# Transformer layer on one core: the shared expert of token tiles 6 and 7 computed behind the expert loop, and the first expert's list between the halves of a product

## What is computed

```python
h = layer_norm(DEEPNORM_ALPHA * h + mix, ln1_g[l], ln1_b[l])
ffn = moe_ffn(h, ...)
h = layer_norm(DEEPNORM_ALPHA * h + ffn, ln2_g[l], ln2_b[l])

def moe_ffn(h, w_router, router_bias, wg, wu, wd, sg, su, sd):
    idx, w = route(xf, w_router, router_bias)          # 6 of 64 experts for each token
    routed = routed_experts(xf, idx, w, wg, wu, wd)    # each expert: (silu(x wg) * (x wu)) wd, weighted
    shared = (jax.nn.silu(xf @ sg) * (xf @ su)) @ sd   # hidden width 256, every token
    return routed + shared
```

## Time and profile before

| | us |
|---|---|
| median of three runs | 2063.84 |
| fastest and slowest of them | 2063.03, 2066.24 |
| the profiled execution's own time | 2066.02 |
| its span, first to last instruction | 2064.2 |
| TensorE busy | 1989.3 (96%) |
| VectorE busy | 1136.6 (55%) |
| GpSimd busy | 777.1 (38%) |
| ScalarE busy | 505.2 (24%) |
| mean granted TensorE clock | 0.989 |

### The profile page before, as it was taken

The page is one execution under the profiler, slowest core; times in us unless marked ns, Lnnn a source line. Parts: engine busy times, 40 slices in busy tenths (PEclk is TensorE's granted clock), DMA queues, the critical chain, the costliest instruction groups (busy, mean ns, idle before and its releaser), DMA issues.

```text
span 2064.2 us, 23774 instructions
## 1 busy us (share of the span) xinstructions
PE 1989.3 (96%) x7237; PEld 1004.3 (49%) x7238; DVE 1136.6 (55%) x3065; ACT 505.2 (24%) x1102; POOL 777.1 (38%) x717
## 2 busy tenths in 40 slices
PE   8999999999999999999999999999999999999991
PEld 6444667575544444444445554444444444444440
DVE  6222546776611222235676656966666656666645
ACT  3111554452322222224432230111111111111113
POOL 1762005612122222115980003554554545454531
PEclk9999999999999999999999999999999999999996
DMA  5421000011141222144353006999999999999964
GB/s 147 132 87 41 21 21 22 22 47 47 46 138 69 74 77 77 57 130 161 111 202 141 31 32 260 369 364 359 360 360 354 364 346 354 347 342 352 337 206 171
DMA packets 129639, 370.45 MB, mean 179 GB/s; under 512 B 33712, under 2 KB 65668, under 8 KB 103832
## 3 DMA queue, kind: packets, MB, share of 16 engines
q1 hardware_dynamic: 103960, 314.83, 41.1%
q0 software_dynamic: 23520, 54.61, 10.5%
q10 hardware_dynamic: 2080, 0.01, 0.1%
HBM read 320.57 MB, written 68.17 MB: 188 GB/s over the span
## 4 chain that ended last, share of the span: by engine, by line
PE 25%; DMA 21%; issue 4%; POOL 3%; DVE 2%; POOLq 0%; ACT 0%; SPq 0%; DVEq 0%
DMA sums<-arena,row_to 21%; PE banks L3193 8%; PE banks L2289 4%; PE banks L3209 3%; PE banks L2336 3%; POOL arena L2136 2%; PE banks L2014 2%; PE banks L279 1%; PE banks L2352 1%; PE banks L2312 1%; DMA arena<-in_w_router_dram 0%; DVE arena L3269 0%; PE banks L3201 0%; DVE arena L3186 0%; PE banks L2299 0%
## 5 line engine op out<-in xcount | busy, mean ns | idle before, releaser
L3193 PE MATMUL banks<-arena 128*128 128x512 f32 x1056 | 466.6, 595 | 4.1 <-issue 3.5
L3172 POOL DMA_INDIRECT arena<-h_rows,index x268 | 281.0, 1048 | 140.2 <-issue 78.7
L3193 PEld LDWEIGHTS banks<-arena 128*128 128x128 f32 x1056 | 196.6, 191 | 227.7 <-issue 227.6
L1720 PE MATMUL banks<-arena 128*128 128x512 f32 x672 | 298.8, 594 | 0.4 <-ACT arena L323 0.4
L3209 PE MATMUL banks<-arena 128*128 128x512 f32 x528 | 237.5, 592 | 1.4 <-ACT arena L3008 0.9
L3180 POOL DMA_INDIRECT sums<-arena,row_to x66 | 106.2, 1609 | 275.9 <-DMA sums<-arena,row_to 242.2
L279 PE MATMUL banks<-arena 128*128 128x512 f32 x416 | 193.5, 602 | 2.3 <-PEq L108 2.2
L1720 PEld LDWEIGHTS banks<-arena 128*128 128x128 f32 x672 | 123.2, 190 | 134.7 <-issue 134.7
L3156 DVE TENSOR_SCALAR index<-row 32x1 uint32<-32x1 f32 x1072 | 155.4, 145 | 17.1
L3209 PEld LDWEIGHTS banks<-arena 128*128 128x128 f32 x528 | 100.2, 190 | 127.1 <-issue 125.3
L3186 DVE STREAM_TRANSPOSE arena<-arena 128x1024 f32<-128x1024 f32 x66 | 133.7, 2026 | 48.9 <-PE banks L3193 47.2
(11 more groups left out here) (400 smaller groups left out, 2420.0 us busy)
## 6 DMA issues: line engine op xcount, KB each, us to landing
arena<-in_w_exp_gate_dram SPq DMA_DIRECT2D x66, 1024.0 KB, 6.4
arena<-in_w_exp_up_dram SPq DMA_DIRECT2D x66, 1024.0 KB, 10.7
arena<-in_w_exp_down_dram SPq DMA_DIRECT2D x66, 1024.0 KB, 13.5
arena<-in_w_in_dram SPq DMA_DIRECT2D x26, 1024.0 KB, 5.4
gates<-arena SPq DMA_DIRECT2D x60, 256.0 KB, 2.0
arena<-gates SPq DMA_DIRECT2D x15, 1024.0 KB, 7.7
arena<-h_rows,index POOLq DMA_INDIRECT x268
arena<-in_x_dram SPq DMA_DIRECT2D x8, 512.0 KB, 5.6
```

What stands on the lines that cost most here:

```text
L1720: mm = pe.matmul(gate_bank(n, b), left[:, k, :], right[:, k, :], start=(alone and k == 0), stop=(k == 3), skip_group_check=True)
L3172: return pool.indirect_dma_start(w.x[k][:, 256 * q:256 * (q + 1)], None, rows, bass.IndirectOffsetOnAxis(ap=g.index[:, k, q:q + 1], axis=0 ...
L3193: mm = pe.matmul(g.bank[:, 2, :].rearrange("p (a f) -> p a f", a=2), xT[:, k, :], wgu[:, :, k, :], start=(k == 0), stop=(k == KT - 1))
```

## The change

Tiles 6 and 7 (`EARLY` = 6 and up) have their shared expert no longer ahead of the expert loop but in `finish`.

- `up`, `turn_hidden`, `down` on TensorE, `gate`, `turned_hidden` on ScalarE and `hidden`, `sum_base` on VectorE are gone for these tiles. `last_down` and `last_sum` are now those of tile 5.
- In their place ScalarE multiplies the rows of tiles 6 and 7 by ALPHA (`scale`, two instructions), and SyncE stores these. The order of the stores changes to 0, 1, 2, 3, 6, 7, 4, 5. Those of tiles 0 and 1 signal `kept_free`, the other six `sums_begun`.
- The turned rows of tiles 6 and 7 must live until the end. They are written to the rows of tiles 0 and 1 in `base` (`late_turned`), so `turned(6)` and `turned(7)` wait for `kept_free`. The shared weights stay too. The overflow tables and the gain and bias rows of the last normalisation, which lay over the weights, move over other rows of `base`. So VectorE waits for all six stores (`sums_begun`) before each quarter of `overflow_tables`, and SyncE waits for them before the loads of gain and bias.
- The list of expert 0 stands between the two halves of `up(5)`; `index(0)` comes before `hidden(5)`. List 3 moves from before the first product of expert 0 to behind it, and step 0 on VectorE is written in another order: it turns the rows of expert 1 and makes `hidden` first, then index 3 and select 4.
- In `finish` TensorE computes both `up` as soon as it has left the loops, then for each late tile `turn_hidden`, the tile's rows of `sums` times the identity into the banks, and `down` added to them. ScalarE reads the sum of tiles 6 and 7 out of the banks. Its Silu, and copies of the turned hidden product, stand between the normalisation of the tiles.

```diff
 LAG = 3
+EARLY = NT - 2
+KEPT = BASE
+TABLES = BASE + 2 * D
...
         def begin_sum(m):
-            sp.wait_ge(s["base"], m + 1)
-            sp.dma_start(g.sums[m * P:(m + 1) * P, :], base[:, m, :]).then_inc(g.sums_begun, 16)
+            if m < EARLY:
+                sp.wait_ge(s["base"], m + 1)
+            else:
+                sp.wait_ge(s["scaled"], m - EARLY + 1)
+            sp.dma_start(g.sums[m * P:(m + 1) * P, :], base[:, m, :]).then_inc(
+                kept_free[m] if m < NT - EARLY else g.sums_begun, 16)
...
-        for m in range(NT - DELAY - 1, NT - 2):
+        begin_sum(NT - DELAY - 1)
+        for m in range(EARLY, NT):
             begin_sum(m)
-        sp.wait_ge(s["gu"], NT)
+        sp.wait_ge(s["gu"], EARLY)
         load_expert(g, sp, 2)
-        begin_sum(NT - 2)
-        sp.wait_ge(s["dn"], NT)
+        begin_sum(EARLY - 2)
+        sp.wait_ge(s["dn"], EARLY)
         load_expert(g, sp, 3)
-        begin_sum(NT - 1)
+        begin_sum(EARLY - 1)
...
-        up(5)
+        up(5, range(0, KT // 2))
         lists(0)
+        up(5, range(KT // 2, KT))
         down(4)
         turn_hidden(5)
-        up(6)
         lists(1)
-        down(5)
-        turn_hidden(6)
-        up(7)
         lists(2)
-        down(6)
-        turn_hidden(7)
-        first.last_down = lambda: down(NT - 1)
+        first.last_down = lambda: down(EARLY - 1)
...
+        index(0)
         hidden(5)
-        index(0)
         select(1)
         sum_base(4)
-        hidden(6)
         index(1)
         select(2)
-        sum_base(5)
         turned_first()
+        index(2)
         select(3)
-        hidden(7)
-        index(2)
-        sum_base(6)
-        first.last_sum = lambda: sum_base(NT - 1)
+        first.last_sum = lambda: sum_base(EARLY - 1)
...
+            if m >= EARLY:
+                act.wait_ge(kept_free[m - EARLY], 16)
...
+        def scale(m):
+            act.wait_ge(h1_stored[m], 16)
+            act.activation(base[:, m, :], base[:, m, :], ACT.Copy, scale=ALPHA).then_inc(s["scaled"], 1)
...
+        for m in range(EARLY, NT):
+            scale(m)
         turned_hidden(4)
         gate(5)
         turned_hidden(5)
-        gate(6)
-        turned_hidden(6)
-        gate(7)
-        turned_hidden(7)
...
-    ovhot = g.region(R1, 48, NE)
+    ovhot = g.region(TABLES, 48, NE)
...
+            sp.wait_ge(g.sums_begun, 16 * EARLY)
...
-                lists(0, 3)
 
             def step(i, c):
                 up(i, c)
+                if not has(i, c, -2):
+                    lists(i, c + 3)
                 if has(i, c, -1):
                     down(i, c - 1)
                 else:
                     first.last_down()
-                if has(i, c, 4):
+                if has(i, c, 4) and has(i, c, -1):
                     lists(i, c + 4)
                 turn_hidden(i, c)
...
+            last.tensor(pe, picked[-1])
...
-                if has(i, c, -1):
+                if not has(i, c, -1):
+                    turned(i, c + 1)
+                    hidden(i, c)
+                    index(i, c + 3)
+                    select(i, c + 4)
+                else:
                     take_rows(i, c - 1)
-                if has(i, c, 3):
-                    index(i, c + 3)
-                if has(i, c, 4):
-                    select(i, c + 4)
-                if has(i, c, 1):
-                    turned(i, c + 1)
-                hidden(i, c)
+                    if has(i, c, 3):
+                        index(i, c + 3)
+                    if has(i, c, 4):
+                        select(i, c + 4)
+                    if has(i, c, 1):
+                        turned(i, c + 1)
+                    hidden(i, c)
                 if has(i, c, -1):
                     result(i, c - 1)
                 else:
                     first.last_sum()
                 if isinstance(i, int) and i == 0:
+                    dve.wait_ge(g.sums_begun, 16 * EARLY)
                     overflow_tables(g, dve, c, then, s["tabled"])
...
-                    pool.wait_ge(g.sums_begun, 16 * NT)
+                    pool.wait_ge(g.sums_begun, 16 * EARLY)
...
+def late_turned(g, m):
+    return g.region(KEPT + D * (m - EARLY), KT, P)
...
+    def tensor(pe, count):
+        pe.wait_ge(v["list"], count)
+        for m in late:
+            for k in range(KT):
+                mm = pe.matmul(bank[:, up_bank[m], :], late_turned(g, m)[:, k, :], wgu[:, k, :],
+                               start=(k == 0), stop=(k == KT - 1))
+            mm.then_inc(s["gu"], 1)
+        for i, m in enumerate(late):
+            pe.wait_ge(s["hid"], i + 1)
+            for k in range(2):
+                mm = pe.transpose(bank[:, up_bank[m], k * P:(k + 1) * P], hid[:, k * P:(k + 1) * P], g.ident[:])
+            mm.then_inc(s["hT"], 1)
+            pe.wait_ge(sum_in[m], 32)
+            for h in range(2):
+                pe.matmul(bank[:, sum_bank[m] + h, :], g.ident[:], z(m)[:, h * HALF:(h + 1) * HALF],
+                          start=True, stop=False)
+            pe.wait_ge(s["hTr"], i + 1)
+            for h in range(2):
+                for k in range(2):
+                    mm = pe.matmul(bank[:, sum_bank[m] + h, :], hidT[:, k, :], wdn[:, k, h * HALF:(h + 1) * HALF],
+                                   start=False, stop=(k == 1))
+            mm.then_inc(s["dn"], 1)
...
+        def late_hidden(i):
+            dve.wait_ge(s["si"], i + 1)
+            if i:
+                dve.wait_ge(s["hT"], i)
+            dve.tensor_tensor(hid, silu, bank[:, up_bank[late[i]], FF:], ALU.mult).then_inc(s["hid"], 1)
...
+            if m == 2:
+                late_hidden(1)
...
+        def late_gate(i):
+            act.wait_ge(s["gu"], i + 1)
+            if i:
+                act.wait_ge(s["hid"], i)
+            act.activation(silu, bank[:, up_bank[late[i]], 0:FF], ACT.Silu).then_inc(s["si"], 1)
+
+        def late_hidden(i):
+            act.wait_ge(s["hT"], i + 1)
+            if i:
+                act.wait_ge(s["dn"], i)
+            act.activation(hidT.rearrange("p k n -> p (k n)"), bank[:, up_bank[late[i]], 0:FF],
+                           ACT.Copy).then_inc(s["hTr"], 1)
+
+        late_gate(0)
         for m in range(1, NT):
-            act.wait_ge(sum_in[m], 16)
-            act.activation(scratch[0], z[:, m, :], ACT.Copy, accum_out=total[:, m:m + 1]).then_inc(s["to"], 1)
+            if m == 2:
+                late_gate(1)
+                late_hidden(0)
+            if m == 4:
+                late_hidden(1)
+            if m < EARLY:
+                act.wait_ge(sum_in[m], 32)
+            else:
+                act.wait_ge(s["dn"], m - EARLY + 1)
+            act.activation(scratch[0] if m < EARLY else z(m), z(m) if m < EARLY else total_of(m), ACT.Copy, accum_out=total[:, m:m + 1]).then_inc(s["to"], 1)
             deviation(m - 1)
             act.wait_ge(s["me"], m + 1)
```

53 lines of the change are left out of this document (33 added, 20 removed).

## The result

The changed kernel takes **2074.54 us** (median of 5 runs, 2071.02 to 2075.29) where the kernel before, on the same chip, takes 2063.84 (5 runs, 2062.57 to 2066.77). The medians are 10.7 us apart; the ratio that is used here, from all runs, is 1.0044, with a 95% interval of 1.003 to 1.0059, so 9 us slower (6 to 12). The forecast was 2066.0, with a range up to 2072 and a chance of 0.34 for slower. The prediction was **wrong**: it held a time within 0.2% of before for the likeliest, and the time lies outside its range. Two of its terms came out too small, the one for the start of the loop and the one for the time behind it.

A forecast was written before the change was run, and what follows sets the result against it. The prediction took the chain of scatters, 11.09 us apart, to bound the kernel, its end set by the first scatters. Loop -0.7 and tail +2.9 gave +2.2 us on 2063.84, so 2066.0, range 2060 to 2072.

The forecast's parts named there:

- What bounds the kernel: Expert loop: scatters wait for one another, 11.09 us apart; its end is set by when the first scatters were early.
- Index 0 and the first rows: Hand-over: index 0 ends 4.0 us earlier; expert 0's slowed gather takes 6.1 us, rows in at 1265.7.
- T: Hand-over: the time when expert 0's gathered rows are transposed, forecast 1267.7 (ends 1265.5 and 1269).
- TensorE's clock: Hand-over: idle time drops TensorE to half clock, adding 1.9 us to the expert product behind each gap.
- The store that VectorE waits for: Hand-over: VectorE stands 8 us until tile 5's store lands, 12.2 us after expert 3's load is issued.
- H: Marker of the loop's start: end of expert 1's `hidden` on VectorE, 1302.84 before, forecast 1303.5, 0.7 later.
- The scatters' slack: First scatters: 3.0 of 3.8 us lost there before come back, so the loop starts and ends 0.7 earlier.
- no slack: Rival, chance 0.28: scatter latency does not shrink, +2.3 reaches the end, 2069.0; decided if expert 1's scatter issues after 1320.
- Behind the loop: After the loop: +2.9 us, from table loads and a second hidden product, with tile 6's `down` just hidden; ends +2.7 and +5.5.
- dear tail: Rival behind the loop, chance 0.06: table switches cost twice their load or the second turned product comes late; +2.6, 2068.6.
- Transfers unhindered: Rival at the hand-over, chance 0.10: the gather takes 2.3 us and the store lands 2.6 after its issue; 2058.4.
- TensorE's work counts in full: Rival, chance 0.03: all 21.6 us of products removed from TensorE are gained, plus 2.9 behind the loop; 2045.

The follow-up runs named there:

- e8: Changed kernel with expert 0's list again behind the whole of `up(5)` and its index work behind `hidden(5)`; ratio 1.0059 to the kernel before.
- e3: Changed kernel with Copy in place of Silu for the gates of tiles 6 and 7, dropping two table loads; ratio 1.0043 to the kernel before.
- e2: Changed kernel with the `sums` rows of tiles 6 and 7 loaded third and fourth behind the loop; ratio 1.003 to the kernel before.
- e12: Kernel before plus an unread Silu and copy on ScalarE between tiles 1 and 2 behind the loop, forcing two table loads; 2068.39 against 2065.44 us, ratio 1.0017.
- e6: Kernel before with only expert 0's list between the halves of `up(5)` and its index work ahead of `hidden(5)`; ratio 0.9993.
- e4b: Changed kernel with nine unread TensorE products before the first expert product and twelve behind expert 0's first down product; ratio 1.0041 to the kernel before.
- e5: Changed kernel with the edits of e1 and e2 together; ratio 1.0007 to the kernel before.
- e10: Changed kernel with three small overflow-table vectors moved off tile 5's rows, VectorE and SyncE's gain and bias loads awaiting five stores; ratio 1.0006 to the kernel before.
- e11: Changed kernel with the edits of e9 and e10 together; 2061.5 against 2065.57 us for the kernel before, ratio 0.9981.
- e13: Changed kernel with nine unread TensorE products during the wait for tile 6's rows behind the loop; ratio 1.0052 to the kernel before.
- e14: Changed kernel with four unread TensorE products during the wait for tile 6's rows behind the loop; ratio 1.0056 to the kernel before.
- e9: e5 with tile 6's work up to its turned hidden put back ahead of the loop, `up(6)` in TensorE's gap; 2063.44 against 2065.97 us before, ratio 0.9988.
- e1: Changed kernel with SyncE storing tile 5's sums before issuing expert 3's weight loads; ratio 1.0018 to the kernel before.

## Why the prediction was wrong, step by step

**What bounds the kernel: right, with less to spare than it says.** Scatters wait for each other from the fifth on, and the loop's end moves with the first of them: across the table, scatter 4 spans 100.1 to 111.3 and the last scatter 772.6 to 787.3, in nearly the same order. But TensorE is close behind: from the fourth step on it works for over 180 us without a pause, 10.83 us for an expert in both kernels, against the scatters' 11.09. And of the scatters of the earlier trace rows the one at 1498.35 was not released by the one before it, as the text has it, but by VectorE's transpose (its own bracket says so); before's last chain of waits runs through TensorE's products up to there and only then through the scatters, in the changed kernel through the scatters from 1345.72 on.

**Index 0 and the first rows: right.** Forecast T was 1267.7, 20.3 us behind `up(5)`; it is 20.4. e8 shows the list's part, 3.9 (forecast 4.0). The gather was slow, as taken: the fourth one is issued at 1260.88 and the rows are in at 1267.19, 6.3 us later (forecast 6.1).

**TensorE's clock: right in kind.** +1.9 was forecast for each product behind a gap; measured +2.2 and +2.0.

**The store that VectorE waits for: right in kind, 1.5 us too small in H.** H should have been 56.1 behind `up(5)` and is 57.6. The store landed 13.1 us behind the load's issue, where I took 12.2 from a row of before; the issue itself came 0.6 later than forecast (33.4 against 32.8), half of that by the slower product. By the Trainium skill (DMA: Bandwidth & Descriptors, "Anatomy of one DMA"), with its fixed cost behind the last byte, H would have been 1.3 later than forecast, and the trace agrees better with that than with my figure: 13.1 here, 13.0 and 13.2 in e3 and e2. The section describes GpSimd's DMAs, and this store is SyncE's, so the agreement is in size only. I had argued the cost away with a store on an idle queue.

**The scatters' slack: the first step that failed.** The sentence is "I take that 3.0 of the 3.8 come back". Without slack the loop would start as much later as H (2.2) and the slower step behind it (13.0 us from transpose to transpose on TensorE in place of 11.4, so 1.6): 3.8 in all. The scatter of expert 1 is in fact only 0.1 later than before, counted from `up(5)`, so the slow gather was indeed gone; the mark that I had set, that scatter issued after 1320, was met (1321.09) by the trace's shift of 1.4 alone. But it did not last. The slow product of expert 2 made the next scatter 1.1 late, scatter 4 is 0.7 late, and then two steps of 12.2 us make scatter 9 3.1 late (165.3 against 162.2). By the groups of the table the loop ends 3.0 later. So 0.8 of the 3.8 came back and not 3.0, and the rival "no slack", with its chance of 0.28, was nearer than my figure. What lengthened the two steps is open; in each a scatter landed 11.3 or 11.4 us behind its start, where its neighbours took 10.3.

The loop's part was forecast at -0.7 and is +3.0: 1.5 by the late H, 2.2 by the slack.

**Behind the loop: the second step that failed.** +2.9 was forecast, +5.9 came. The table loads are as forecast (e12: +2.8). The failing sentence is "the `down` products of tile 6 need its rows (about 2042), start after 4 us of idle TensorE at half clock, and end about 2048.1; ScalarE wants the next turned product at 2048.4: just hidden". I had spaced the rows by the 1.2 us between the first two; over seven tiles they come 1.5 apart in the changed kernel (0.52 MB take 1.4 us at the 376 GB/s that all queues moved from 2036 to 2046). The first rows are in at 3.3 us behind the first load, tile 6's at 12.2 (forecast 10.7). And at half clock the 12 passes took 8.1 us and not 6.1. Both went the same way, by 1.5 and 2.0, against a slack of 0.3 by my own numbers: the wait of 3.2. A term that is "just hidden" with 0.3 to spare, behind two estimates of a microsecond each, should have been entered with half its cost: the bound of +5.5 stood in the text, with a chance of only 0.06 in "dear tail". Of the wait of TensorE for `sums` rows the last paragraph said that it would make the prediction wrong, and so it did.

**The sum.** Loop end +3.0 by the groups and behind +5.9 give +8.9 us in place of the forecast's +2.2, and the timed ratio says +9 (6 to 12). The pair of profiles alone gives less, +1.3 and +5.9, and what is missing lies in before's profile, whose execution was 2.2 us over its median: from scatter 9 to the last it took 617.1 us, where its two like (e6, e12) took 615.0 and 613.5 and the changed kernel 615.3. The same sum (a row's last scatter less 777.5, its "behind" less 29.8) comes within a microsecond of the timed ratio in e2, e3, e4b, e5, e10 and e11 and misses it by 1.4 to 4.2 in the others; each is one profile. In e13 and e14 the timed runs are 2.5 and 4.2 us over it, and that I can't place.

**The other rivals.** "Transfers unhindered" fell: the gather and the store were both slowed, as the earlier trace rows said. "TensorE's work counts in full" fell: of the 21.6 us of products removed nothing reached H, which came 2.2 later, since VectorE's chain of list, index, gather and transpose, and then the store, took their place.

## What to carry to other kernels

Work taken off an engine is worth what the next chain behind it allows, so look first for what that engine will wait for instead; here the freed gap of TensorE was best used by putting part of the removed work back into it (e9, e11), which in e9 kept its clock too. A buffer that is laid over rows on their way out turns their store into a wait of the engine that writes next: put small vectors elsewhere, and issue such a store ahead of any bulk load on its queue. Where one function's table is needed between two uses of another, count both loads at full price, and where a wait comes out as "just hidden", add the clock that the waiting engine loses.

## What the runs showed of the hardware

TensorE's clock behind an idle time of some 2.5 to 6 us came out either way, and the length of the idle time does not order the price. The first expert product, 7.03 us at full clock, took 7.13 behind an idle time of 2.53 (e9) and 10.03 behind one of 2.98 (e11), each with a product of 7.1 us and a short list ahead of it; without the filled gap it took 10.07 behind 4.42 (e1) and 8.54 behind 6.22 (e8). Behind the loop the 12 passes took 5.4 us behind 3.78 of idle time (e10), 8.1 behind 4.26 (changed kernel), 6.9 behind 5.89 (e4b) and 7.1 behind 2.55 (e14). So a gap costs nothing or up to 3 us here, and executions of the same code differ by that.

A store of 512 KB landed 3.8 us behind its own issue where it was ahead of the weights on its queue (e1), and 8.7 to 10.6 behind it where 3.1 MB of weights, issued 4 us ahead, were still passing (e13 the least, e4b the most).

A load of ScalarE's table cost its 1.28 us and no more in these traces: in e12 the Silu starts 0.01 us behind its end, and two loads with their two small instructions made the time behind the loop 2.8 us longer, and the program 2.95 by the timed medians (2 to 5 by the ratio).
